# Parameter loads of the S5 and mixer parts behind later chunks' weights, the gate copy ahead of the rounding, tables and b blocks moved

## The chip, the cores and the metric

One core of a Trainium2 chip. A core has TensorE (PE, matrix products into PSUM), VectorE (DVE), ScalarE (ACT), GpSimd (POOL) and SyncE (SP), which here issues every DMA. Each engine runs its own list of instructions in order; they wait for each other by semaphores. The metric is the device time of one execution in microseconds (us), less is better.

## What is computed

A two-layer trunk over 256 positions of width 1024, in float32. Each layer has three sub-layers: a SwiGLU FFN, four token mixers side by side, and a second FFN:

```
mod = silu(c) @ ada_w[l] + ada_b[l]            # shift, scale, gate for each of 3 sub-layers
u = x*(1+scale0) + shift0;  x = LN(alpha*x + 0.5*gate0*(silu(u@w1)*(u@w3))@w2)
u = x*(1+scale1) + shift1;  x = LN(alpha*x + gate1*([A|B|C|D](u@w_in))@w_out)
u = x*(1+scale2) + shift2;  x = LN(alpha*x + 0.5*gate2*FFN(u))
```

Mixer D is an S5 state-space block. From its parameters (lam_re, lam_im, log_step, b_re, b_im, c_re, c_im) the kernel derives decays, tables of cosines and sines for 128 positions, and the matrices B and C. These depend on parameters alone, so they are worked out on DVE during the first FFN of the layer. Mixers A and B use sinks, w_uq and w_iq; mixer C uses the gate biases; D's output uses glu_w.

## The kernel before, in words

**The FFN.** Eleven chunks of 256 hidden columns (`CHUNKS`). Products are split: each float32 factor is a rounded part and a remainder, and PE does three products (high*high, high*low, low*high; lines 520 to 522 for the input weights, 545, 548, 549 for the output weights). For chunk c+1 the input weights come by DMA into a two-slot ring (`load_ffn_in`, 2 DMAs of 1 MB), ACT rounds them (`w_in_high`, L1610), DVE takes the remainder (`w_in_low`, L1013). The same goes for the output weights (`load_ffn_out`, `w_out_high` L1618, `w_out_low` L1018). The silu (ACT, L1603) and the product and split of h (DVE `ffn_tile`, L1002 to L1007) lie between PE's input and output matmuls. A chunk has two halves, ft = 0 and 1.

**adaLN blocks.** The modulation for later sub-layers is computed beside the FFN: in a chunk DVE multiplies a 2 MB block of `ada_w` by silu(c) in eight steps into `acc` (L935 or L938, and L941), and PE sums over partitions in the next chunk, before its output matmuls (L494 for columns, L503 for gates, which land in PSUM bank 7). ACT then copies a gate out (`copy_gate`, L1597). In layer 0 there is a block in each chunk 0 to 10 (the last in two halves, in chunk 10), in layer 1 in chunks 0 to 4 and 7 to 9.

**Orders around the change.** All orders are written out by hand.
- SP: weights of chunk 1, adaLN block, then 24 parameter DMAs on the semaphore `params_loaded` (L369 to L392), then `load_beside(0, ch)` for ch = 1 to 10: weights of chunk ch+1, each behind a wait for its ring slot, and the adaLN block of ch, behind a wait for DVE to have finished the block before. For ch = 9 in layer 0 SP also waits for the last table operation (`rot_step`), because half an adaLN block is loaded over the tables' scratch.
- PE: after chunk 1 it waits for the first gate and for all 24 parameter loads, and turns the rows of `prow` (L579). After chunk 10 it turns the b blocks (L586) and the c blocks (L593) and then the normalised x (L485).
- ACT in `ffn_chunk`: silu and input rounding of both halves, output rounding of the next chunk (behind a wait for PE's last matmul of this chunk), gate copy.
- DVE: behind each chunk's own work a piece of the S5 parameters: angles in 2, poles in 3, tables from 4 on (`TABLE_AT`; seven doubling steps of six operations), inverse in 4, gains in 5, `c_blocks` in 3 (layer 0) or 5 (layer 1), and `b_blocks` after the last h of chunk 10, in front of `deepnorm`. In layer 1 chunks 0 to 3 also carry the residual of the layer before (L1085, L1088).

## Time and profile before

| | us |
|---|---|
| median of 3 runs | 1149.54 (1148.61 to 1151.38) |
| profiled execution | 1149.38 |
| its span, first to last instruction | 1147.1 |
| PE busy | 1059.2 |
| DVE busy | 904.5 |
| ACT busy | 422.5 |

Times in the trace count from the first instruction of the span. A chunk of the first FFN takes PE close to 17.8 us. Layer 0's first FFN runs from about 38 to 250 us, layer 1's from about 601 to 797 us.

### The profile page before, as it was taken

How to read it: one execution, taken by the hardware profiler on the slowest of the kernel's cores; microseconds unless marked ns; L12 is line 12 of the kernel's file. 1: busy time of each engine (PE TensorE's matmuls, PEld its weight loads, DVE VectorE, ACT ScalarE, POOL GpSimd, SP SyncE). 2: the span in 40 equal slices, each digit the busy share in tenths (PEclk: the TensorE clock that was granted, in tenths of full speed). 3: DMA queues.
4: the chain of work that ended last, by engine and by line, in shares of the span. 5: the costliest groups of instructions: out<-in, count | busy, mean ns of one | idle time of the engine just before them, and what ended most of it. 6: DMA issues, size and time to landing. Idle time of an engine off the chain costs nothing.

```text
span 1147.1 us, 16956 instructions
## 1 busy us (share of the span) xinstructions
PE 1059.2 (92%) x6865; PEld 931.6 (81%) x6865; DVE 904.5 (79%) x1498; ACT 422.5 (37%) x566; POOL 38.9 (3%) x56
## 2 busy tenths in 40 slices
PE   1979999979999799999979999998899979999994
PEld 1869999967875599999969999997687549999994
DVE  6787999989975789878878898698697577755555
ACT  0435333311463333333333553332246243333330
POOL 1000000003000100000000000000300010000000
PEclk9999999988999899999989999999899989999997
DMA  9897989685251568888966886786134246654640
GB/s 367 266 313 259 330 277 307 225 219 187 80 199 57 183 236 313 290 274 308 330 231 186 300 282 217 255 316 153 73 128 165 92 157 210 220 180 155 217 147 37
DMA packets 184504, 250.82 MB, mean 219 GB/s; under 512 B 25372, under 2 KB 133216, under 8 KB 183404
## 3 DMA queue, kind: packets, MB, share of 16 engines
q1 hardware_dynamic: 184428, 249.76, 63.8%
q8 instruction: 54, 0.88, 0.3%
q14 instruction: 22, 0.18, 0.0%
HBM read 248.69 MB, written 1.05 MB: 218 GB/s over the span
## 4 chain that ended last, share of the span: by engine, by line
PE 82%; DVE 8%; SPq 5%; issue 2%; ACT 2%; DMA 1%; POOL 0%; POOLq 0%; DVEq 0%; ACTq 0%
PE PS L520 14%; PE PS L521 14%; PE PS L522 14%; PE PS L617 9%; PE PS L545 6%; PE PS L549 6%; PE PS L548 6%; PE PS L846 2%; PE PS L624 2%; PE PS L702 2%; SPq L323 2%; PE PS L494 1%; DVE stats L1062 1%; DVE xn L1057 1%; DVE xn L1050 1%
## 5 line engine op out<-in xcount | busy, mean ns | idle before, releaser
L520 PE MATMUL PS<-u_hi,w_in_hi 128*128 128x256 f32 x1408 | 400.3, 284 | 7.2 <-DVE u_lo L972 4.4
L522 PE MATMUL PS<-u_hi,w_in_lo 128*128 128x256 f32 x1408 | 400.5, 284 | 0.0
L521 PE MATMUL PS<-u_lo,w_in_hi 128*128 128x256 f32 x1408 | 400.0, 284 | 0.0
L520 PEld LDWEIGHTS PS<-u_hi,w_in_hi 128*128 128x128 f32 x1408 | 271.2, 193 | 10.1 <-issue 5.5
L521 PEld LDWEIGHTS PS<-u_lo,w_in_hi 128*128 128x128 f32 x1408 | 269.9, 192 | 1.6
L522 PEld LDWEIGHTS PS<-u_hi,w_in_lo 128*128 128x128 f32 x1408 | 269.5, 191 | 0.0
L1013 DVE TENSOR_TENSOR w_in_lo<-w_in_ring,w_in_hi 128x2048 fp32r<-128x2048 f32 x88 | 201.5, 2290 | 39.6 <-ACT w_in_hi L1610 39.5
L1610 ACT ACTIVATE w_in_hi<-w_in_ring 128x2048 fp32r<-128x2048 f32 x88 | 168.0, 1913 | 7.0 <-DMA w_in_ring<-in_ffn_w_dram 7.0
L941 DVE SCALAR_TENSOR_TENSOR acc<-arena,cs,acc 128x512 f32<-128x512 f32 x210 | 157.9, 752 | 7.5
L545 PE MATMUL PS<-w_out_hi,h_parts 128*128 128x512 f32 x352 | 146.6, 417 | 6.7 <-DVE h_parts L1007 6.6
L1618 ACT ACTIVATE w_out_hi<-w_out_ring 128x1024 fp32r<-128x1024 f32 x88 | 88.6, 1054 | 162.7 <-PE PS L549 162.7
L1603 ACT ACTIVATE arena<-PS 128x256 f32<-128x256 f32 x88 | 33.8, 384 | 300.3 <-PE PS L522 300.3
L549 PE MATMUL PS<-w_out_hi,h_parts 128*128 128x512 f32 x352 | 139.7, 397 | 0.0
L548 PE MATMUL PS<-w_out_lo,h_parts 128*128 128x512 f32 x352 | 139.5, 396 | 0.0
L1018 DVE TENSOR_TENSOR w_out_lo<-w_out_ring,w_out_hi 128x1024 fp32r<-128x1024 f32 x88 | 103.7, 1219 | 17.1 <-ACT w_out_hi L1618 16.9
L1002 DVE TENSOR_TENSOR arena<-arena,PS 128x256 f32<-128x256 f32 x88 | 36.8, 418 | 85.9 <-ACT arena L1603 85.8
L617 PE MATMUL PS<-uT,w_in_ring 128*128 128x256 f32 (+1 forms) x416 | 99.3, 397 | 3.6 <-ACT uT L1579 2.5
L617 PEld LDWEIGHTS PS<-uT,w_in_ring 128*128 128x128 f32 (+1 forms) x416 | 80.6, 197 | 20.0 <-issue 4.5
L545 PEld LDWEIGHTS PS<-w_out_hi,h_parts 128*128 128x128 f32 x352 | 66.8, 190 | 24.2 <-issue 10.7
L548 PEld LDWEIGHTS PS<-w_out_lo,h_parts 128*128 128x128 f32 x352 | 66.8, 190 | 16.6 <-issue 2.9
L549 PEld LDWEIGHTS PS<-w_out_hi,h_parts 128*128 128x128 f32 x352 | 66.9, 190 | 16.2
L1852 POOL TENSOR_TENSOR rstd<-var_eps,neg_half 128x1 f32<-128x1 f32 x12 | 10.5, 875 | 907.9 <-DVE var_eps L1067 907.9
(286 smaller groups left out, 988.1 us busy)
## 6 DMA issues: line engine op xcount, KB each, us to landing
w_in_ring<-in_ffn_w_dram SPq DMA_DIRECT2D x88, 1024.0 KB, 7.7
arena<-in_ada_w_dram SPq DMA_DIRECT2D x30, 2048.0 KB, 8.3
w_out_ring<-in_ffn_w_dram SPq DMA_DIRECT2D x44, 1024.0 KB, 6.5
w_in_ring<-in_w_in_dram SPq DMA_DIRECT2D x6, 1024.0 KB, 6.6
w_in_ring<-in_w_in_dram SPq DMA_DIRECT2D x10, 512.0 KB, 5.1
w_out_ring<-in_w_out_dram SPq DMA_DIRECT2D x4, 1024.0 KB, 10.6
w_in_ring<-in_w_in_dram SPq DMA_DIRECT2D x2, 2048.0 KB, 8.7
w_in_ring<-in_w_out_dram SPq DMA_DIRECT2D x4, 1024.0 KB, 5.9
```

The source lines that it names most:

```text
L520: pe.matmul(y, hi, u_hi[:, kt, :], start=(i == 0), stop=False)
L521: pe.matmul(y, hi, u_lo[:, kt, :], start=False, stop=False)
L522: mm = pe.matmul(y, lo[:, kt, half, :], u_hi[:, kt, :], start=False, stop=(i == KT - 1))
L545: mm = pe.matmul(y, h_hi, w_out_hi[ft][:, cols], start=(first and ft == 0), stop=False)
L548: pe.matmul(y, h_hi, w_out_lo[slot][:, ft, cols], start=False, stop=False)
L549: mm = pe.matmul(y, h_lo, w_out_hi[ft][:, cols], start=False, stop=(last and ft == 1))
L617: mm = pe.matmul(o[0:w, :], w_in_ring[(G_MIX + m) % 2][:, kt, c0:c0 + w], uT[:, kt, :], start=(kt == 0), stop=(kt == KT - 1))
L941: v.scalar_tensor_tensor(acc[:, :], part(buf, t), cs[:, t:t + 1], acc[:, :], ALU.mult, ALU.add).then_inc(sem("acc_step"), 1)
L1013: v.tensor_tensor(w_in_tile(w_in_lo, slot, ft), w_in_tile(w_in_ring, slot, ft), w_in_hi[ft][:, :, :, :].bitcast(F32), ALU.subtract).then_i ...
L1018: v.tensor_tensor(w_out_lo[slot][:, ft, :], w_out_ring[slot][:, ft, :], w_out_hi[ft][:, :].bitcast(F32), ALU.subtract).then_inc(sem("w_out ...
L1610: a.activation(w_in_hi[ft][:, :, :, :], w_in_tile(w_in_ring, slot, ft), ACT.Copy).then_inc(sem("w_in_high"), 1)
L1618: a.activation(w_out_hi[ft][:, :], w_out_ring[slot][:, ft, :], ACT.Copy).then_inc(sem("w_out_high"), 1)
```

## The change

The 24 parameter loads are split. Eleven (the rows of `prow` and `log_dt`) stay where they were. The four c loads go behind chunk loads 3 and 4 (two each), the two b loads behind 5 and 6, and the seven others (glu, uq, iq, sinks twice, two gate biases) behind 7. PE's transpose after chunk 1 waits for eleven loads only. Waits for all 24 are added in front of the mixer on PE, in `b_blocks`, `c_blocks`, in front of the sink logits on DVE and in front of the gate biases on ACT. ACT copies a gate before the output rounding and not after it. Each table step is done one chunk earlier, behind the poles in chunk 3; `c_blocks` and `b_blocks` are both done in chunk 9.

```diff
--- before.py
+++ after.py
@@ -73,7 +73,7 @@
 
 
 R_LNG, R_LNB, R_CW, R_CB, R_MHG, R_DS, R_GB, R_LR, R_LI, ROWS = 0, 24, 48, 64, 68, 70, 72, 74, 82, 90
-PARAM_DMAS = 24
+FIRST_PARAM_DMAS, PARAM_DMAS = 11, 24
 
 AW = 512
 BLOCKS = 9 * D // AW
@@ -377,22 +377,32 @@
                     sp.dma_start(log_dt[64 * half:64 * half + 64, :],
                                  log_step[L].rearrange("o (i two) -> two (o i)", two=2)[half:half + 1].to_broadcast([64, 8]),
                                  allow_slow_non_contiguous=True).then_inc(pl, 16)
-                for k, src in enumerate((b_re, b_im)):
-                    sp.dma_start(b_raw[:, k, :, :], src[L].rearrange("o (i two) p c -> (two p) (o i) c", two=2)).then_inc(pl, 16)
-                for k, src in enumerate((c_re, c_im)):
-                    for rep in range(2):
-                        sp.dma_start(c_blk[:, k, :, rep * 64:(rep + 1) * 64],
-                                     src[L].rearrange("o (t g) c p -> (g c) (o t) p", t=2)).then_inc(pl, 16)
-                sp.dma_start(glu_sb[:, :, :], glu_w[L].rearrange("o (t p) n -> p (o t) n", p=P)).then_inc(pl, 16)
-                sp.dma_start(uq_sb[:, :], w_uq[L].rearrange("o p n -> p (o n)")).then_inc(pl, 16)
-                sp.dma_start(iq_sb[:, :], w_iq[L].rearrange("o p n -> p (o n)")).then_inc(pl, 16)
-                for k in range(2):
-                    sp.dma_start(sinks_sb[:, k, :], sinks[L].to_broadcast([P, H])).then_inc(pl, 16)
-                for k, src in enumerate((ig_b, fg_b)):
-                    sp.dma_start(gate_bias[:, k:k + 1], src[L].rearrange("o h -> h o")).then_inc(pl, 16)
+                def load_blocks(k):
+
+                    if k < 2:
+                        for rep in range(2):
+                            sp.dma_start(c_blk[:, k, :, rep * 64:(rep + 1) * 64],
+                                         (c_re, c_im)[k][L].rearrange("o (t g) c p -> (g c) (o t) p", t=2)).then_inc(pl, 16)
+                    else:
+                        sp.dma_start(b_raw[:, k - 2, :, :], (b_re, b_im)[k - 2][L].rearrange("o (i two) p c -> (two p) (o i) c", two=2)
+                                     ).then_inc(pl, 16)
+
+                def load_mixer_params():
+
+                    sp.dma_start(glu_sb[:, :, :], glu_w[L].rearrange("o (t p) n -> p (o t) n", p=P)).then_inc(pl, 16)
+                    sp.dma_start(uq_sb[:, :], w_uq[L].rearrange("o p n -> p (o n)")).then_inc(pl, 16)
+                    sp.dma_start(iq_sb[:, :], w_iq[L].rearrange("o p n -> p (o n)")).then_inc(pl, 16)
+                    for k in range(2):
+                        sp.dma_start(sinks_sb[:, k, :], sinks[L].to_broadcast([P, H])).then_inc(pl, 16)
+                    for k, src in enumerate((ig_b, fg_b)):
+                        sp.dma_start(gate_bias[:, k:k + 1], src[L].rearrange("o h -> h o")).then_inc(pl, 16)
 
                 for ch in range(1, CHUNKS):
                     load_beside(0, ch)
+                    if 3 <= ch < 7:
+                        load_blocks(ch - 3)
+                    if ch == 7:
+                        load_mixer_params()
                 sp.wait_ge(sem("x_ready"), l * 6 + 2)
                 waited(sp)
                 load_ln(l, 0)
@@ -575,7 +585,7 @@
                     ffn_chunk(l, 0, c)
                     if c == 1:
                         pe.wait_ge(sem("gate_ready"), (1, 8)[l])
-                        pe.wait_ge(sem("params_loaded"), (l + 1) * (16 * PARAM_DMAS))
+                        pe.wait_ge(sem("params_loaded"), 16 * (l * PARAM_DMAS + FIRST_PARAM_DMAS))
                         pe.transpose(PS[:, 7, 0:ROWS], prow[:, :], ident[0:ROWS, 0:ROWS]).then_inc(sem("prm_turned"), 1)
                 release_out(0)
 
@@ -704,6 +714,7 @@
                     if k == 1:
                         pe.drain().then_inc(sem(f"w_out_used{g % 2}"), 1)
 
+                pe.wait_ge(sem("params_loaded"), (l + 1) * 16 * PARAM_DMAS)
                 chunk_in(0)
                 z_feature("ud0", 0, 0)
                 z_feature("cq", 0, 256)
@@ -1164,6 +1175,7 @@
 
                 def b_blocks():
 
+                    v.wait_ge(sem("params_loaded"), (l + 1) * 16 * PARAM_DMAS)
                     kre = S5["k_re"].unsqueeze(2).to_broadcast([P, 8, 16])
                     kim = S5["k_im"].unsqueeze(2).to_broadcast([P, 8, 16])
                     bt = [qk_tanh[:, k * P:(k + 1) * P].rearrange("p (i c) -> p i c", c=16) for k in range(4)]
@@ -1180,6 +1192,7 @@
 
                 def c_blocks():
 
+                    v.wait_ge(sem("params_loaded"), (l + 1) * 16 * PARAM_DMAS)
                     for k, sign in ((0, 1.0), (1, -1.0)):
                         v.scalar_tensor_tensor(c_blk[:, k, :, :], c_blk[:, k, :, :], sign,
                                                block_mask[:, :].unsqueeze(1).to_broadcast([P, 2, P]), ALU.mult, ALU.mult
@@ -1207,21 +1220,24 @@
                             v.wait_ge(sem("rot_step"), at + 4)
                             v.tensor_tensor(sin_t[:, :, hi], t4[2], t4[3], ALU.add).then_inc(sem("rot_step"), 1)
 
-                TABLE_AT = {4: ((0, range(6)), (1, range(6))), 5: ((2, range(6)), (3, range(6))), 6: ((4, range(6)),),
-                            7: ((5, range(6)),), 8: ((6, range(0, 3)),), 9: ((6, range(3, 6)),)}
+                TABLE_AT = {3: ((0, range(6)), (1, range(6))), 4: ((2, range(6)), (3, range(6))), 5: ((4, range(6)),),
+                            6: ((5, range(6)),), 7: ((6, range(0, 3)),), 8: ((6, range(3, 6)),)}
 
                 for c in range(CHUNKS - 1):
                     ffn_chunk(l, 0, c)
                     if l and c < 4:
                         residual(l - 1, 2, c)
+                    if c == 3:
+                        s5_poles()
                     for k, ops in TABLE_AT.get(c, ()):
                         table_ops(k, ops)
                     if c == 4:
                         s5_inverse()
                     if c == 5:
                         s5_gains()
-                    if c == (3, 5)[l]:
+                    if c == 9:
                         c_blocks()
+                        b_blocks()
                     if c == 0 and l == 0:
                         bias_constants()
                     if c == 1:
@@ -1229,8 +1245,6 @@
                         v.tensor_copy(prm[:, :], PS[:, 7, 0:ROWS]).then_inc(sem("prm_ready"), 1)
                     if c == 2:
                         s5_angles()
-                    if c == 3:
-                        s5_poles()
 
                 tile = ff_tile(l, 0, CHUNKS - 1)
                 for ft in range(2):
@@ -1239,7 +1253,6 @@
                     if l == 0:
                         ada_block(10, None, "ada_halves_loaded", ft + 1, acc_2, ts=range(4 * ft, 4 * ft + 4))
                     ffn_tile(ft, tile)
-                b_blocks()
                 assert step[0] == STEPS
                 if l == 0:
                     mod_cols(2, 4, 6, 8, 10)
@@ -1432,6 +1445,7 @@
                                                ALU.mult, ALU.add).then_inc(sem("conv_step"), 1)
 
                 s5_rotate_out(1)
+                v.wait_ge(sem("params_loaded"), (l + 1) * 16 * PARAM_DMAS)
                 sk = sinks_sb[:, :, :].rearrange("p t h -> p (t h)")
                 v.wait_ge(sem("consts_ready"), 8)
                 logits(bias_a, work[2], "sa_ready", "sa_read", mx_a, nmx_a, "a", sk)
@@ -1629,8 +1643,10 @@
                             a.wait_ge(sem(f"w_in_loaded{1 - slot}"), in_loads(l, ff_group(f, c + 1)))
                         w_in_high(1 - slot, ft, tile + (2 + ft))
                 if not last:
+                    if c - 1 in ADA[l, f] and gate_of(ADA[l, f][c - 1]) is not None:
+                        copy_gate(ADA[l, f][c - 1])
                     w_out_high(l, f, c + 1)
-                if c - 1 in ADA[l, f] and gate_of(ADA[l, f][c - 1]) is not None:
+                elif c - 1 in ADA[l, f] and gate_of(ADA[l, f][c - 1]) is not None:
                     copy_gate(ADA[l, f][c - 1])
 
             evac_uT(0, 0, 1, 0, lambda: w_in_high(0, 0, 0))
@@ -1717,6 +1733,7 @@
                 z_copies("ka", [(kaT[64 * k:64 * k + 64, t, :], 64 * t, 64 * t + 64) for t in range(2) for k in range(2)])
                 a.wait_ge(sem("x_ready"), l * 6 + 4)
                 a.wait_ge(sem("gates_turned"), l + 1)
+                a.wait_ge(sem("params_loaded"), (l + 1) * 16 * PARAM_DMAS)
                 for k in range(2):
                     a.activation(rows[:, k, :], PS[0:H, 6, k * T:(k + 1) * T], ACT.Identity, bias=gate_bias[:, k:k + 1]
                                  ).then_inc(sem("gates_read"), 1)
```

## Rows read from the trace of the kernel before

**Rows 1.** The page: busy time, share of the span and instructions of each engine.
```profile
PE 1059.2 (92%) x6865; PEld 931.6 (81%) x6865; DVE 904.5 (79%) x1498; ACT 422.5 (37%) x566; POOL 38.9 (3%) x56
```

**Rows 2.** Chain of waits: start us, us, what; layer 0's first sub-layer.
```profile
61.79 8.77 DMA w_in_ring<-in_ffn_w_dram
...
185.59 0.86 PE PS L503 x2
203.34 0.86 PE PS L503 x2
```

**Rows 3.** Order of SP: start us, us spent issuing, line, what; [idle, releaser] in all orders.
```profile
44.47 2.42 SPq L381 DMA_DIRECT2D b_raw<-in_b_re_dram  x1
...
61.35 1.02 SPq L323 DMA_DIRECT2D w_in_ring<-in_ffn_w_dram  x2
...
64.75 0.76 SPq L293 DMA_DIRECT2D arena<-in_ada_w_dram  x1
...
168.97 1.00 SPq L323 DMA_DIRECT2D w_in_ring<-in_ffn_w_dram  x2
```

**Rows 4.** Order of ACT in layer 0: start us, us, line, operation.
```profile
70.58 1.92 ACT L1610 ACTIVATE w_in_hi<-w_in_ring 128x2048 fp32r<-128x2048 f32 x1 [7.05 <-DMA w_in_ring<-in_ffn_w_dram]
...
82.67 0.57 ACT L1597 ACTIVATE gate_bc<-PS 128x512 f32<-128x512 f32 x1
...
180.24 1.91 ACT L1610 ACTIVATE w_in_hi<-w_in_ring 128x2048 fp32r<-128x2048 f32 x1
```

**Rows 5.** Order of PE in chunks 0 to 2 of layer 0.
```profile
51.72 0.39 PE L545 MATMUL PS<-w_out_hi,h_parts 128*128 128x512 f32 x1
...
68.62 1.02 PE L503 MATMUL PS<-acc,ones 128*128 128x512 f32 x2
...
76.09 0.47 PE L545 MATMUL PS<-w_out_hi,h_parts 128*128 128x512 f32 x1 [3.67 <-DVE h_parts L1007]
...
83.30 0.30 PE L579 MATMUL PS<-ident,prow 90*128 90x90 f32 x1 [2.64 <-ACT gate_bc L1597]
...
96.35 1.02 PE L503 MATMUL PS<-acc,ones 128*128 128x512 f32 x2
```

**Rows 6.** Windows: stretch, length, busy us of each engine, PEclk, DMA share, GB/s.
```profile
76.00:84.00 8.00, 5.28 (x18) 3.88 (x19) 7.36 (x8) 3.22 (x4) 0.00 (x0) 0.78 1.09 360
```

**Rows 7.** Order of DVE at the adaLN block of chunk 1, layer 0.
```profile
78.57 0.75 DVE L935 SCALAR_TENSOR_TENSOR acc<-arena,cs,gate_bias_row 128x512 f32<-128x512 f32 x1 [0.43 <-DMA arena<-in_ada_w_dram]
```

**Rows 8.** Windows, same columns, while layer 1's parameters are loaded.
```profile
604.00:608.00 4.00, 4.00 (x28) 4.00 (x27) 4.00 (x4) 0.04 (x1) 0.00 (x0) 0.73 0.13 9
```

**Rows 9.** Order of DVE in chunks 4 and 5 of layer 1.
```profile
684.39 0.43 DVE L1007 TENSOR_TENSOR h_parts<-arena,h_parts 128x256 fp32r<-128x256 f32 x1
...
696.17 0.17 DVE L1202 TENSOR_TENSOR rot_flat<-cos_t 128x8 f32<-128x8 f32 x1
...
697.62 0.16 DVE L1149 TENSOR_TENSOR s5p<-prm 128x8 f32<-128x8 f32 x1
...
707.77 0.19 DVE L1202 TENSOR_TENSOR rot_flat<-cos_t 128x32 f32<-128x32 f32 x1
...
711.10 0.76 DVE L1184 SCALAR_TENSOR_TENSOR c_blk<-c_blk,block_mask 128x256 f32<-128x256 f32 x2
```

**Rows 10.** Order of PE: first output matmul of chunk 4, layer 1.
```profile
685.84 0.80 PE L545 MATMUL PS<-w_out_hi,h_parts 128*128 128x512 f32 x1
```

**Rows 11.** Order of DVE at the first deepnorm of either layer.
```profile
243.69 0.28 DVE L1170 TENSOR_TENSOR qk_tanh<-b_raw,s5p 128x128 f32<-128x128 f32 x1
...
246.33 1.29 DVE L1050 TENSOR_TENSOR xn<-PS,gate_bc 128x512 f32<-128x512 f32 x2
...
795.21 1.29 DVE L1050 TENSOR_TENSOR xn<-PS,gate_bc 128x512 f32<-128x512 f32 x2
```

**Rows 12.** Order of PE: the matmul that finishes the second bank, either layer.
```profile
245.84 0.63 PE L549 MATMUL PS<-w_out_hi,h_parts 128*128 128x512 f32 x1
...
793.89 0.39 PE L549 MATMUL PS<-w_out_hi,h_parts 128*128 128x512 f32 x1
```

## The prediction, made before the changed kernel was run

> **What bounds the kernel now.** I read the page first, then the chain of waits, then the orders of SP, PE, ACT and DVE around each place that the diff touches. TensorE is busy for 1059.2 of 1147.1 us [rows 1]. In the first sub-layer (the FFN's eleven chunks) the chain is PE's own work, one chunk every 203.34 - 185.59 = 17.75 us [rows 2]. So the change can pay only where PE waits, and cost only where it makes PE wait. PE's waits near the touched code are three: chunk 1 of layer 0, and the turn from the FFN to the mixer in each layer, where the chain runs over DVE.
>
> The wait in chunk 1 starts at SP. SP begins the thirteen loads that move at 44.47 us and issues chunk 2's first weights behind them, at 61.35 [rows 3]. These land as 61.79 + 8.77 = 70.56 [rows 2]. ACT rounds them in program order between the two silus of chunk 1: it was free 7.05 us before, at 63.53 [rows 4]. DVE stands behind ACT, the second half of h comes late, and PE waits 3.67 us at 76.09. When PE has finished, it waits once more, 2.64 us to 83.30, for the gate copy [rows 5], which ACT runs at 82.67, after the output weights' rounding, and that itself waits for PE's last matmul of the chunk [rows 4]. The granted clock is 1.0 before, and 0.78 on average from 76 to 84 us, after the 3.67 us wait [rows 6]: part of that stretch ran at 1.2 GHz.
>
> **The start of layer 0 (gain).** Without the thirteen loads SP comes to chunk 2's weights at 44.47 and waits for their ring slot, which PE gives back with its first output matmul of chunk 0, at 51.72 [rows 5]. With the slow landing of before (70.58 - 61.35 = 9.2 us [rows 3, 4]) they are there at 61.2, 2.3 us ahead of ACT's 63.53. Before, h's second half was there 76.09 - 70.58 = 5.5 us after ACT began; 5.5 after 63.53 is 69.0, but its silu waits for PE's last input matmul (68.6) and some 2.5 us of silu, weight difference and products follow: 71.2. PE wants it at 76.09 - 3.67 = 72.4: no wait. The gate sum is done by PE at the start of chunk 1's output, so ACT copies the gate at about 71.5 instead of 82.67, and the transpose at 83.30 follows PE's last matmul directly. What is late next? The adaLN block of chunk 1 is issued when DVE has finished block 0, at 62.5; with its old landing time (it was waited for until 78.57 after an issue at 64.75, 13.8 us [rows 3, 7]) it is there at 76.4, DVE finishes its eight steps (6.2) at 82.6 and, with the parameter copy (0.2), the output weights' differences (2.3) and the products (1.1), chunk 2's first h at 86.2. PE wants that half a us after its sum at 86.5 (68.62 + 17.85, below), at 86.9. That is the thinnest cover here, 0.7 us, with the old landing time as the bad end; it lands amid less traffic now, so I take no wait.
> The sum: PE's gate or column sum opens each chunk's output part at 68.62 in chunk 1 and 96.35 in chunk 2 [rows 5], 27.73 us apart. Undisturbed it is 17.75 plus 0.10 for the transpose: 17.85. Gain 9.88 us: 6.31 of waits and 3.57 of slow clock. Bounds: 6.3 if the clock falls all the same, and 9.9, since nothing more is lost there.
>
> **The moved loads where they now stand.** Four c loads behind chunks 3 and 4, b_re and b_im one each behind 5 and 6, seven small ones behind 7. Each follows its chunk's adaLN block, some 8 us ahead of the next weights. They are not free: from 604 to 608 us, when nothing but the b loads of layer 1 was left to move, the 16 DMA engines were busy for 0.13 at 9 GB/s [rows 8], and that state held for some 8.5 us, so 4.3 us of queue for each b load. Weights issued behind one would land up to 4.3 us later. Chunk 8's weights are issued at 168.97 and ACT wants them at 180.24 [rows 3, 4]: 11.3 us, and with an ordinary 7 us to land 4.3 us are left, just the size of the hold; ACT's result is wanted by DVE only 1 us after that. In layer 1 chunks 5 and 6 have no adaLN load. I take 0; the other end is one stall like that of chunk 1.
> The Trainium skill, page "DMA: Bandwidth & Descriptors", section "Why a DMA increments its semaphore by 16 and not by 1", says that one DMA is spread over the largest number of engines up to 16 that divides the slowest dimension of both sides; for b that dimension is 2 in the source, so two engines of 16, 0.125, and the trace's 0.13 agrees. By that rule the weights' sixteen-engine DMAs are held on two engines for the whole of a b load and the rest can't help, which makes the sum the other end above; if b were spread like the weights the hold would be far below 4.3 us.
>
> **Tables one chunk back (DVE).** A pair of table steps costs 697.62 - 696.17 = 1.45 us; the second pair takes 12 instructions of about 0.19, some 2.1 us [rows 9]. Layer 0: chunk 3 gains 1.45 and loses the c masks (0.76 with its end, 0.68 until the next operation starts [rows 9]), chunk 4 gains 0.7, and h has some 2 us of cover there: nothing. Layer 1 has no cover: DVE runs the residual as well. Chunk 3 gets +1.45. Chunk 4's first h was ready at 684.39 + 0.43 = 684.82 and PE used it at 685.84 [rows 9, 10]; now 686.27, a wait of 0.4. DVE runs without a pause there, so its second h comes 3.3 us after the first, and PE's matmuls on the first take 3.2: another 0.1. In chunk 5 DVE is later by 2.1 in all (the next pair goes in where the first one was), h's second half comes 0.4 after the moved PE. Together +1.0 us (bounds 0 and 2.1, all that DVE is late). Chunk 5 has no adaLN block in layer 1 and DVE recovers.
>
> **b blocks and c masks in chunk 9.** The b blocks (8 instructions, about 1.97 us, from 243.69) stood between the last h and deepnorm [rows 11]. Chunk 9 loses the last three table operations (1.93) and gets c masks and b blocks (0.68 + 1.97): +0.72 in both layers.
> Layer 0: DVE is the bound in chunk 10, because two halves of an adaLN block stand in it. So the last h and PE's last output matmuls come 0.72 later. Deepnorm began at 246.33, after the b blocks. Now DVE is free at 245.1, but its second multiply needs the bank that PE finished at 245.84 + 0.63 = 246.47 [rows 11, 12], now 247.2, where DVE had started it at 246.93. Net +0.3 (bounds -1.25, all that DVE is free earlier, and +0.72).
> Layer 1: no adaLN block in chunk 10; DVE waited for PE in front of the last h, which hides the +0.72. DVE is free 1.97 earlier, 793.2 instead of 795.21 [rows 11]. PE's second bank is done at 793.89 + 0.39 = 794.28 [rows 12], the second multiply stood at 795.81: -1.4. What is late next is ACT, whose copies of the turned blocks follow PE and not DVE: they may push the first normalisation, but the chain ends with the second, 3.8 us later, which has room.
> The half block that waited for the last table is issued 17 us earlier, and with it the mixer's first weights; PE did not wait for either, so 0. The new waits for all 24 loads stand 15 us or more behind the last load: 0.
>
> Sum: -9.88 + 1.0 + 0.3 - 1.4 = -9.98, near 10 us. The profiled execution took 1149.38 (span 1147.1 and 2.3 around it); that is 1139.4. The median of the runs is 1149.54, 0.16 above it: I say 1139.5.
>
> **Rivals.**
> 1. The start pays only in part: weights or the adaLN block land later than I let them. For: 0.7 us of cover. Against: SP issues less. About 2 us of wait return: 1141.5. Chance 0.08.
> 2. A b load holds weights once in layer 0. A whole stall like chunk 1's is 3.67 plus up to 3.57 of slow clock, 7.2 us; a partial one 2. 1141.5 to 1146.7. Chance 0.12.
> 3. The gate wait does not go (it was for the loads, not the copy). The copy ended at 83.25 and PE went on at 83.30, which speaks against it. 2.64 and a part of the slow clock, 4.2: 1143.7. Chance 0.05.
> 4. Slower: the b loads hold weights in both layers, at chunks 7 and 8, four places of 7.2 us. It decides from the second whole stall on: 14.4 - 10 = +4.4, 1154. For: each hold is as long as the room. Against: it needs the long landing as well, and the chunks of layer 1 have no adaLN traffic ahead. Chance 0.05.
> 5. It doesn't do what it says: chunk 2's weights can't come earlier since their slot is not free. SP would wait at 52, so this needs a slot given back 9 us later than PE's order has it. 1149. Chance 0.03.
> The forecast has 0.67, with 1137.5 to 1142 for itself. The range 1136.8 to 1145 takes in rivals 1 and 3 and most of 2. A change of 0.3%, 3.4 us, is what a measurement can tell from none: faster 0.92, same 0.03, slower 0.05.
>
> **What would show it.** After: chunk 2's weights issued at about 52 and no wait of ACT for them; no 3.67 and 2.64 us waits of PE; the sums of chunks 1 and 2 17.85 us apart at clock 1.0; PE's chunk 4 of layer 1 waiting about 0.5 us for h; the first multiply of deepnorm after PE's bank and not after b blocks. Wrong: ACT waiting for weights of chunks 7 or 8, or the sums still more than 20 us apart.

## The result and the profile after

The changed kernel takes 1138.45 us (median of 4 runs, 1137.98 to 1139.63) against 1149.07 us for the kernel before, run beside it (4 runs, 1146.81 to 1151.38): a ratio of 0.991, 95% interval 0.9893 to 0.9927. A second set of runs of the same kernel gave 1137.91 (4 runs) against 1148.3, ratio 0.9904 (0.9888 to 0.9921). The forecast was 1139.5. The profiled execution took 1138.35 us, its span 1136.1.

The page after, busy time of each engine. PE's work is the same count of matmuls and 5.8 us shorter than in [rows 1], which fits less of it running at the lower clock; the span is 11.0 us shorter:

```profile
PE 1053.4 (93%) x6865; PEld 926.9 (82%) x6865; DVE 904.4 (80%) x1498; ACT 422.4 (37%) x566; POOL 38.9 (3%) x56
```

Order of SP after (start us, us spent issuing, line, what), for [rows 3]. Chunk 2's weights are issued at 51.70 instead of 61.35; the first moved load stands behind chunk 3's adaLN block:

```profile
42.99 1.31 SPq L377 DMA_DIRECT2D log_dt<-in_log_step_dram  x2
51.70 1.02 SPq L323 DMA_DIRECT2D w_in_ring<-in_ffn_w_dram  x2
...
62.13 0.58 SPq L293 DMA_DIRECT2D arena<-in_ada_w_dram  x1
...
97.28 1.68 SPq L384 DMA_DIRECT2D c_blk<-in_c_re_dram  x1
```

Order of ACT after, for [rows 4]. The 7.05 us wait is now 1.45, and the gate is copied at 70.45 instead of 82.67:

```profile
64.51 1.93 ACT L1624 ACTIVATE w_in_hi<-w_in_ring 128x2048 fp32r<-128x2048 f32 x1 [1.45 <-DMA w_in_ring<-in_ffn_w_dram]
...
70.45 0.58 ACT L1611 ACTIVATE gate_bc<-PS 128x512 f32<-128x512 f32 x1
```

Order of PE after, for [rows 5]: the gate sums of chunks 1 and 2 and the transpose between them. Neither wait is there, and the sums stand 17.88 us apart instead of 27.73:

```profile
68.16 1.02 PE L513 MATMUL PS<-acc,ones 128*128 128x512 f32 x2
...
74.56 0.24 PE L589 MATMUL PS<-ident,prow 90*128 90x90 f32 x1
...
86.04 1.02 PE L513 MATMUL PS<-acc,ones 128*128 128x512 f32 x2
```

Windows after (stretch, length, busy us of PE, PEld, DVE, ACT, POOL, granted clock, DMA share, GB/s), for [rows 6]: the granted clock that was 0.78 is 1.00.

```profile
76.00:84.00 8.00, 8.00 (x70) 8.00 (x69) 7.43 (x11) 5.80 (x6) 0.00 (x0) 1.00 0.95 328
```

The two turns to the mixer, order of DVE after, for [rows 11]. In both layers the first multiply now waits for PE's bank instead of standing behind the b blocks:

```profile
235.39 1.29 DVE L1061 TENSOR_TENSOR xn<-PS,gate_bc 128x512 f32<-128x512 f32 x2 [0.58 <-PE PS L559]
...
784.22 1.29 DVE L1061 TENSOR_TENSOR xn<-PS,gate_bc 128x512 f32<-128x512 f32 x2 [0.77 <-PE PS L559]
```

Where the 11.03 us of span went, by PE's own landmarks (distance between the same two matmuls, after minus before): up to chunk 1's sum -0.46; chunk 1 to chunk 2, -9.85; the end of layer 0's first part and the turn to the mixer, -0.69; the start of layer 1, +0.21; its chunks 4 and 5, +0.93; its turn to the mixer, -1.17. Chunk 1's sum stands anywhere between 66.9 and 69.0 us over all the kernels below, so the first term is start-up spread. A "sum" here is PE's sum of an adaLN block, which opens a chunk's output part; "layer 0's stretch" below is the distance from chunk 10's sum to the first sum of the mixer.

### The profile page after: what moved, and what is told of

It is laid out like the page before. It is cut to its first block, busy times and chain, and to the rows that moved or that the text cites. A ratio compares the mean times of both kernels' runs of the same rounds, so it can differ in the third digit from the quotient of the medians.

```text
span 1136.1 us, 16957 instructions
## 1 busy us (share of the span) xinstructions
PE 1053.4 (93%) x6865; PEld 926.9 (82%) x6865; DVE 904.4 (80%) x1498; ACT 422.4 (37%) x566; POOL 38.9 (3%) x56
## 4 chain that ended last, share of the span: by engine, by line
PE 83%; DVE 10%; issue 2%; ACT 2%; DMA 2%; SPq 0%; POOL 0%; POOLq 0%; DVEq 0%; ACTq 0%
PE PS L530 14%; PE PS L531 14%; PE PS L532 14%; PE PS L627 9%; PE PS L555 6%; PE PS L559 6%; PE PS L558 6%; PE PS L857 2%; PE PS L634 2%; PE PS L712 2%; DVE acc L952 2%; DMA xn<-in_ada_w_dram 2%; PE PS L504 1%; DVE stats L1073 1%; DVE xn L1068 1%
```

## Experiments

Twelve runs were made, in four groups (eleven other kernels, and the changed one again), each group beside the kernel before on one chip (that was 1149.02, 1149.77, 1148.3 and 1148.56 us). "Distance" is always from chunk 1's to chunk 2's sum in layer 0: 27.73 before, 17.88 after, 17.75 for an undisturbed chunk.

**1. The loads alone.** The changed kernel with the gate copy where it was:

```
-                    if c - 1 in ADA[l, f] and gate_of(ADA[l, f][c - 1]) is not None:
-                        copy_gate(ADA[l, f][c - 1])
                     w_out_high(l, f, c + 1)
-                elif c - 1 in ADA[l, f] and ...:
+                if c - 1 in ADA[l, f] and ...:
                     copy_gate(ADA[l, f][c - 1])
```

> The changed kernel with one part undone: ACT copies the gate after the output weights' rounding again. Theory (the wait at PE's transpose is for the copy, and the copy is late since the rounding waits for PE): PE waits 2.6 us before the transpose after chunk 1 of layer 0, and the gate sums of chunks 1 and 2 are 20.5 us apart if the clock stays at 1.0, up to 22 if it falls after the wait (17.88 in the changed kernel); nothing else moves: 1141.0 to 1142.5 us. Rival (the wait was for the parameter loads): no wait, 17.9 us apart, 1138.5 us.

**2. The gate copy alone**: the kernel before with only that edit the other way round.

> The kernel before with the gate copy alone moved ahead of the rounding. Theory: the 2.64 us wait before the transpose goes, the 3.67 us wait for h in chunk 1 stays, and since the clock still falls after it the sums are 23.5 to 25.1 us apart instead of 27.7: 1145.0 to 1146.5 us. Rival (both waits are one and the same lateness of the weights, so that the gain comes only with the loads): the sums stay above 27 us apart, 1149 us.

Measured: the loads alone 1142.63 us (4 runs), ratio 0.9946 (0.9928 to 0.9964); the copy alone 1144.69 (10 runs), ratio 0.9964 (0.9952 to 0.9976). Order of PE, the loads alone:

```profile
66.89 1.02 PE L513 MATMUL PS<-acc,ones 128*128 128x512 f32 x2
...
72.10 0.47 PE L555 MATMUL PS<-w_out_hi,h_parts 128*128 128x512 f32 x1 [1.42 <-DVE h_parts L1018]
...
77.75 0.30 PE L589 MATMUL PS<-ident,prow 90*128 90x90 f32 x1 [2.64 <-ACT gate_bc L1611]
...
90.81 1.02 PE L513 MATMUL PS<-acc,ones 128*128 128x512 f32 x2
```

Order of PE, the copy alone:

```profile
67.64 1.02 PE L503 MATMUL PS<-acc,ones 128*128 128x512 f32 x2
...
76.25 0.72 PE L545 MATMUL PS<-w_out_hi,h_parts 128*128 128x512 f32 x1 [4.82 <-DVE h_parts L1007]
...
92.13 1.02 PE L503 MATMUL PS<-acc,ones 128*128 128x512 f32 x2
```

Each leaves the other's wait: the 2.64 us behind the output matmuls go with the copy and stay with the loads alone, so rival 3 is dead. The distances are 23.92 and 24.49, that is 3.81 and 3.24 gained, while together they gain 9.85. For the first I had expected 20.5 to 22 us and 1142.5 at most, without its 1.42 us wait; the second's distance is inside its 23.5 to 25.1, and its time just under the 1145.0 expected. What each distance has over 17.75, in us: PE's two waits, and the rest, which is the slow clock and some 0.1 of transpose.

| | waits | rest |
|---|---|---|
| before | 6.31 | 3.67 |
| loads alone | 4.06 | 2.11 |
| copy alone | 4.82 | 1.92 |
| both | 0 | 0.13 |

So of the 2.8 us that neither gets alone, 2.6 are waits: 1.42 us for h that the first has and the profiled changed kernel has not, and 1.15 us by which the second's wait is longer than the 3.67 of before. The slow clock goes in two nearly equal parts, with the first wait and with the last.

The 1.42 us come from ACT. Its order in the first of the two:

```profile
66.60 1.92 ACT L1624 ACTIVATE w_in_hi<-w_in_ring 128x2048 fp32r<-128x2048 f32 x1 [4.80 <-DMA w_in_ring<-in_ffn_w_dram]
```

Its weights were issued at 50.48 and came 16.1 us later. In the changed kernel it is 12.8 (51.70 to 64.51), in its second profile 14.9 (50.80 to 65.74), there with a PE wait of 0.25. Over the seven profiles with log_dt in this place they were issued between 50.48 and 52.59 and taken between 64.34 and 66.60: 11.8 to 16.1 us, by and large the longer the earlier they were issued. I had taken 9.2. What holds them?

**3. b loads alone deferred** (the kernel before with b_re and b_im behind chunks 5 and 6, PE's transpose waiting for the other 22), and **4. both b loads behind chunk 5** in the changed kernel:

```
                 for ch in range(1, CHUNKS):
                     load_beside(0, ch)
+                    if ch in (5, 6):                      # 3: in the kernel before
+                        sp.dma_start(b_raw[:, ch - 5, :, :], ...).then_inc(pl, 16)
...
+                    if ch == 5:                           # 4: in the changed kernel
+                        load_blocks(2)
+                        load_blocks(3)
```

> The kernel before with only the two b loads taken from SP's list and put behind chunks 5 and 6; c and mixer loads, gate copy, tables and b blocks as before. Theory of the prediction (the b loads hold the queue, 4.3 us each): the c loads are issued without delay, SP comes to chunk 2's weights near 52, the 3.67 us wait goes, the gate wait stays: sums 20.5 to 22 us apart, 1142 to 1143.5 us. Rival (the two log_dt loads hold one DMA engine for about 8 us, as the share of 0.05 from 590 to 598 us in the changed kernel suggests, and SP is blocked on that engine's ring): the first c load still blocks for some us and the weights are issued at 54 to 58; little of the 3.67 us wait may be left all the same.

> The changed kernel with both b loads behind chunk 5 (c loads behind 3 and 4, the seven others behind 7, as changed). Theory of the prediction (4.3 us of queue for each b load): 8.6 us of hold ahead of chunk 7's weights, which are issued 8 us later; they land about 7 us late, ACT waits for them some 3 us in chunk 6 of layer 0 and PE up to 3 us: 1138.5 to 1143. Rival (a b load costs the queue 2 us or less, and what held it was log_dt): no wait of ACT for weights there, 1138.5 us, no difference from the changed kernel.

Measured: 1143.94 us (6 runs), ratio 0.996 (0.9945 to 0.9975), and 1139.89 (4 runs), ratio 0.9918 (0.9899 to 0.9937). Order of SP in the first, where no b load stands in front of the weights:

```profile
42.92 1.31 SPq L377 DMA_DIRECT2D log_dt<-in_log_step_dram  x2
44.27 3.44 SPq L382 DMA_DIRECT2D c_blk<-in_c_re_dram  x2
47.75 2.38 SPq L382 DMA_DIRECT2D c_blk<-in_c_im_dram  x2
...
50.69 2.95 SPq L385 DMA_DIRECT2D uq_sb<-in_w_uq_dram  x1
...
57.05 1.02 SPq L323 DMA_DIRECT2D w_in_ring<-in_ffn_w_dram  x2
```

The weights go out 4.3 us earlier than the 61.35 of before, for both b loads and not for each; the other 5.35 us to the changed kernel's 51.70 are the c and the seven small loads. SP is still held behind log_dt: issuing uq takes it 2.95 us here and 0.61 in the changed kernel at 170.12, c_im 2.38 against 1.14. ACT waits 3.02 us for the weights (to 66.69) and PE no longer for h: the 3.67 us are gone with the b loads alone, the gate's 2.64 stay, and the distance is 22.19, a little over the 20.5 to 22 expected, with 1.80 of slow clock.

In the other kernel the two b loads went out at 132.10 and 132.79 (the second kept SP for 3.72 us), chunk 7's weights at 140.08, and ACT took those at 151.32 without a wait, against the 3 us of the theory. So b loads do occupy the queue for a few us, but not up to the next weights. Two lines of windows of the changed kernel show one by itself: b_re went out at 682.49 in layer 1, beside megabytes of weights, and by 688 nothing was left to move:

```profile
686.00:688.00 2.00, 2.00 (x20) 2.00 (x19) 1.82 (x10) 0.30 (x2) 0.00 (x0) 1.00 0.57 120
688.00:690.00 2.00, 2.00 (x20) 2.00 (x19) 1.76 (x12) 1.89 (x2) 0.00 (x0) 1.00 0.01 1
```

Windows of the changed kernel at the parameter loads of layer 1, where log_dt went out at 583.59 and no b load is near (same columns as above):

```profile
592.00:594.00 2.00, 2.00 (x11) 2.00 (x11) 2.00 (x4) 1.04 (x2) 0.00 (x0) 0.50 0.05 0
594.00:596.00 2.00, 2.00 (x15) 2.00 (x14) 2.00 (x2) 0.00 (x0) 0.00 (x0) 0.73 0.05 0
596.00:598.00 2.00, 2.00 (x19) 2.00 (x18) 2.00 (x2) 0.00 (x0) 0.00 (x0) 1.00 0.03 0
```

A near-empty state like that of [rows 8], which I put down to the b loads, is here without them, from 590 until 598, 14 us after log_dt's issue. And the 0.13 of [rows 8] is a mean of unlike parts. The same stretch in the kernel before, by 2 us:

```profile
604.00:606.00 2.00, 2.00 (x12) 2.00 (x11) 2.00 (x2) 0.04 (x1) 0.00 (x0) 0.50 0.07 3
606.00:608.00 2.00, 2.00 (x18) 2.00 (x18) 2.00 (x3) 0.00 (x0) 0.00 (x0) 0.97 0.20 14
```

Log_dt is two loads of 512 separate 4-byte numbers each.

**5. log_dt behind chunk 2's weights**, in the changed kernel, counted apart from the other parameters, with ACT's exponential waiting for them:

```
                 for ch in range(1, CHUNKS):
                     load_beside(0, ch)
+                    if ch == 1:
+                        for half in range(2):
+                            sp.dma_start(log_dt[64 * half:64 * half + 64, :], ...)
```

> The changed kernel with log_dt's two small loads issued behind chunk 2's weights, on a semaphore of their own. Theory (the two loads of 4-byte elements hold one of the 16 engines for some 8 us, and the weights behind them wait for that one): chunk 2's weights land about 7 us after their issue instead of 12.8, ScalarE's wait of 1.45 us for them goes, the stretch at 5 to 15% DMA share moves from 50 to 56 us to behind chunk 2's weights, and chunk 3's weights, issued 15 us later, land as before. The time stays 1138.5 within 0.4 us, since TensorE did not wait for these weights. Rival (the weights are slow by themselves, being many small rows at a busy time): they land 12.8 us after their issue again.

Measured: 1145.65 us (7 runs), ratio 0.9967 (0.9956 to 0.9978). Order of SP:

```profile
63.85 1.41 SPq L400 DMA_DIRECT2D log_dt<-in_log_step_dram  x2
70.02 6.07 SPq L323 DMA_DIRECT2D w_in_ring<-in_ffn_w_dram  x2
76.20 5.22 SPq L331 DMA_DIRECT2D w_out_ring<-in_ffn_w_dram  x1
```

Windows, order of ACT and order of PE there:

```profile
70.00:76.00 6.00, 6.00 (x31) 5.00 (x30) 5.83 (x9) 2.21 (x3) 0.00 (x0) 1.00 0.10 18
```

```profile
88.23 1.92 ACT L1625 ACTIVATE w_in_hi<-w_in_ring 128x2048 fp32r<-128x2048 f32 x1 [3.71 <-DMA w_in_ring<-in_ffn_w_dram]
```

```profile
86.55 1.02 PE L514 MATMUL PS<-acc,ones 128*128 128x512 f32 x2
...
93.75 0.47 PE L556 MATMUL PS<-w_out_hi,h_parts 128*128 128x512 f32 x1 [3.39 <-DVE h_parts L1019]
```

The place of the hold moved with log_dt, as said: chunk 2's weights are no longer waited for, and chunk 3's are, which ACT takes 18.2 us after issue. ACT also waits 3.98 us, until 81.33, for log_dt itself, and in layer 1 until 637.48 after an issue at 620.55: 17.5 and 16.9 us from issue to landing, the only direct measures of it. That the time would stay was wrong: log_dt was put six us ahead of weights that were needed, where it had stood nine us ahead of them. PE lost 5.2 us between the sums of chunks 2 and 3 of layer 0 and 4.2 at the same place of layer 1.

**6. log_dt in one piece**: 16 adjacent numbers for each partition, 128 pieces of 64 bytes, and two half-height exponentials that pick the even and the odd ones:

```
-        log_dt = sb("log_dt", [P, 8])
+        log_dt = sb("log_dt", [P, 16])
...
-                                 log_step[L].rearrange("o (i two) -> two (o i)", two=2)[half:half + 1].to_broadcast([64, 8]),
-                                 allow_slow_non_contiguous=True).then_inc(pl, 16)
+                                 log_step[L].to_broadcast([64, 16])).then_inc(pl, 16)
```

> The changed kernel with log_dt loaded as 16 adjacent numbers per partition (128 pieces of 64 bytes instead of 1024 of 4 bytes) and the even and odd ones picked by two half-height exponentials instead of one. Theory (the count of small pieces is what holds an engine and the queue): the stretch at a DMA share of 5 to 15% from 50 to 56 us goes, chunk 2's weights land some 7 to 10 us after their issue instead of 12.8, ScalarE does not wait for them, and the same in layer 1. One more ScalarE instruction of 0.2 us. The time stays at 1138.5 within 0.5 us, since TensorE did not wait there. Rival (the broadcast over the partitions is slow, whatever the pieces): share and landing stay.

Measured: 1143.58 us (6 runs), ratio 0.9955 (0.9939 to 0.9971), beside the second set of the changed kernel at 1137.91. The two kernels in the window where that load was in flight, first this one, then the changed kernel:

```profile
52.00:54.00 2.00, 2.00 (x11) 1.60 (x10) 1.37 (x3) 1.10 (x1) 0.00 (x0) 1.00 0.70 212
54.00:56.00 2.00, 2.00 (x10) 1.64 (x9) 2.00 (x2) 0.00 (x0) 0.00 (x0) 1.00 1.08 374
```

```profile
52.00:54.00 2.00, 2.00 (x10) 1.60 (x9) 1.33 (x4) 1.60 (x1) 0.00 (x0) 1.00 0.27 19
54.00:56.00 2.00, 2.00 (x10) 1.63 (x9) 2.00 (x2) 0.00 (x0) 0.00 (x0) 1.00 0.31 48
```

The hold is gone: the queue runs at full rate 3 us after the weights' issue (51.21), and ACT takes them at 62.52 with no wait. So log_dt's 4-byte pieces are the cause of this hold, and the broadcast, which is still there, is not; whether it is their number, their size or the gaps between them in memory, this run does not tell apart. Yet the time rose by 5.7 us, and not there: an undisturbed feed-forward chunk takes 17.88 to 17.94 us, in every part of the program, instead of 17.74 to 17.84. The last experiment below is about that.

**7. The tables back, 8. the b blocks back, 9. the blocks apart.** The changed kernel with layer 1's tables one chunk later; with b_blocks after the last h; and the first of these with layer 0's c and b blocks in chunks 7 and 8:

```
+                if l:                                              # 7 and 9
+                    TABLE_AT = {c + 1: k for c, k in TABLE_AT.items()}
...
-                        b_blocks()                                 # 8: in chunk 9
...
+                b_blocks()                                         # 8: after the last h
...
-                    if c == 9:                                     # 9
+                    if c == (7, 9)[l]:
                         c_blocks()
+                    if c == (8, 9)[l]:
                         b_blocks()
```

> The changed kernel with layer 1's rotation tables one chunk later, where they stood before (4 to 9 instead of 3 to 8). Theory: of the 0.93 us that layer 1's chunks 4 and 5 lost, all is the tables ahead of chunk 3's and 4's last h tiles, so the distance from chunk 2's sum to chunk 5's sum in layer 1 goes from 54.11 back to some 53.3 us, and the time from 1138.45 to about 1137.5 us. The price: VectorE gets 1.93 us more in chunk 9, so that its h tile for chunk 10 comes at 781.3 us of the changed kernel's clock instead of 779.4, just when TensorE wants it (781.4): a wait of 0 to 0.3 us. Rival (the 0.93 us is start-up spread or b_im's load in chunk 6): the distance stays 54.1 us and the time 1138.5.

> The changed kernel with the b blocks again after the last h tile, the c blocks staying in chunk 9. Theory: layer 1's end gives its 1.17 us back (the first multiply behind the last matmul starts 1.97 us later), so this kernel is about 1.2 us slower there; in layer 0 the last h tile comes 1.97 us earlier, TensorE's wait of 2.51 us before it shrinks to about 0.6 us, and VectorE then does the b blocks before the first multiply, which comes out within 0.5 us of where it is: about 1139.6 us in all. Rival (the 1.17 us come from elsewhere in the end of the layer): the stretch from chunk 10's sum to the transposes behind it in layer 1 stays at 49.5 us and the time at 1138.5.

> The previous kernel but one (tables of layer 1 as before the change) and, in layer 0 alone, the c blocks in chunk 7 and the b blocks in chunk 8; layer 1 keeps both in chunk 9. Theory: in layer 0 VectorE's last h tiles are late by the blocks that stand in chunk 9, 2.69 us; with them out of chunks 9 and 10 TensorE's wait of 2.51 us before the last output tile goes, if chunks 7 and 8 have room for 0.72 and 1.97 us. Layer 0's end gets 1.6 to 2.5 us shorter, and with layer 1's 0.9 us the time is about 1136. Rival (chunks 7 and 8 of layer 0 are as tight as chunk 9, for VectorE works without a gap through them): the lateness is carried along, the wait stays 2.5 us, and the time is 1137.5 as with the tables alone.

Measured: 1138.79 us (4 runs), ratio 0.9901 (0.9885 to 0.9917); 1135.16 (5 runs, 1134.41 to 1139.79), ratio 0.9887 (0.9869 to 0.9905); 1134.35 (4 runs, 1131.73 to 1136.59), ratio 0.9868 (0.985 to 0.9887).

With the tables back, layer 1's stretch from chunk 2's to chunk 5's sum is 53.32 us instead of 54.11, and 53.28 before: 0.79 of the 0.93 us is theirs, the theory's way. The price was as forecast too: from chunk 10's sum of layer 1 to the transposes behind the mixer's start it is 49.80 us, against 49.49 and 49.30 in the two profiles of the changed kernel. The whole time can't show what is left, 0.5 us being under a third of the interval's half width. The profiled execution was even 1.5 us longer, and 1.0 of that is in layer 0's stretch, where this kernel is the changed one to the letter. Order of PE at the last h there, and windows behind it; first with the tables back, then the changed kernel:

```profile
235.23 0.76 PE L555 MATMUL PS<-w_out_hi,h_parts 128*128 128x512 f32 x1 [2.52 <-DVE h_parts L1018]
```

```profile
235.00:237.00 2.00, 1.77 (x4) 1.49 (x5) 0.67 (x7) 0.00 (x0) 0.00 (x0) 0.50 0.99 123
```

```profile
234.33 0.47 PE L555 MATMUL PS<-w_out_hi,h_parts 128*128 128x512 f32 x1 [2.51 <-DVE h_parts L1018]
```

```profile
234.00:236.00 2.00, 1.67 (x7) 1.42 (x8) 1.35 (x7) 0.00 (x0) 0.00 (x0) 1.00 1.06 142
```

The same code, the same wait to a hundredth, and once the granted clock is 0.50 (1.2 GHz) and once 1.00 (2.4 GHz). From chunk 10's sum to the mixer's first sum of this layer that makes 45.73 us in the one and 44.72 in the other; from chunk 10's sum to PE's transpose of the b blocks alone, 11.95 and 10.53.

With the b blocks back, the same stretch of layer 1 (sum to transposes) is 50.38 us against 49.49 in the changed kernel and 49.30 in its second profile: +0.9 to 1.1 where I expected 1.17. In layer 0 PE's wait for the last h is 1.47 instead of 0.79 + 2.51, and the stretch 44.53 against 44.72. These two stretches thus say about 0.7 us slower; but its whole span is 1135.8, as in the changed kernel's two profiles (1136.1 and 1135.5), and its median of 1135.16 is far under the 1139.6 expected, on 5 runs that spread over 5.4 us. The interval just holds the changed kernel's second ratio, 0.9904, and not its first, 0.991. For the whole time this one is inconclusive, and that the b blocks' new place is worth something in the whole is not shown.

With the blocks apart, layer 0's stretch is 42.55 us, 2.17 under the changed kernel, inside the 1.6 to 2.5 forecast: chunks 7 and 8 had the room, PE's waits of 0.79 and 2.51 shrink to one of 1.77 (I had written that it goes), and the clock stays at 1.00. Layer 1 keeps the 0.8 of the tables and pays 0.3 at its end.

**10. The changed kernel again, 11. blocks apart with log_dt in one piece, 12. the same with addresses kept.** The last differs from the one before it in two lines:

```
-        log_dt = sb("log_dt", [P, 16])
+        log_dt_unused = sb("log_dt_unused", [P, 8])
...
         small = sb("small", [P, 32, 8])
+        log_dt = sb("log_dt", [P, 16])
```

> The changed kernel once more, beside the next two on one chip, for the blocks apart and for the short loads of log_dt to be compared with it. It should come out at 1138.5 within 1 us. Where its profile shows the wait of 2.51 us for the last h tile of layer 0's first feed-forward part, the clock behind it is either 1.00 or 0.5 to 0.6; the stretch from chunk 10's sum to the turn of the b blocks is 10.5 us in the first case and 11.4 to 12.0 in the second, as in the runs so far.

> The kernel with layer 1's tables as before, layer 0's c and b blocks in chunks 7 and 8, and log_dt loaded in one piece. Theory: the blocks apart are worth 2.2 us in layer 0 and 0.8 in layer 1 over the changed kernel, less 0.3 at layer 1's end, and the short loads nothing: 1135.5 to 1136 us, or 2.6 us under the changed kernel run beside it. Rival (the runs of the blocks apart were low by chance): less than 1 us under it.

> The previous kernel (blocks apart, log_dt in one piece) with its 16-wide buffer placed behind all others in SBUF and the old 8-wide one left where it was, unused, so that every other buffer has the address that it has in the kernel before the change. Theory (the chunks of 17.90 to 17.93 us instead of 17.75 to 17.84, in every feed-forward part, come from the 32 bytes by which the wider buffer shifted the operands behind it): the chunks go back to 17.75 and 17.84, TensorE's matmuls on u_lo from 285 to 283 ns, and the time from 1139.9 to about 1135.5 us. Rival (the added ScalarE instruction or another change of the program does it): chunks of 17.9 and 1140 us again.

Measured: the changed kernel 1137.91 us, with the clock behind the 2.51 us wait at 1.00 and 10.54 us from chunk 10's sum to the transpose of the b blocks, the first of the two cases; blocks apart with the wider buffer 1139.86 (6 runs), ratio 0.9923 (0.9909 to 0.9937); with the addresses kept 1135.22 (5 runs, 1131.43 to 1136.39), ratio 0.9873 (0.9856 to 0.9891). Groups of PE's instructions (busy us, mean ns), the matmuls on u_lo, first with the addresses shifted, then kept:

```profile
L530 PE MATMUL PS<-u_lo,w_in_hi 128*128 128x256 f32 x1408 | 401.5, 285 | 0.0
```

```profile
L531 PE MATMUL PS<-u_lo,w_in_hi 128*128 128x256 f32 x1408 | 398.4, 283 | 0.0
```

The program is the same and only addresses differ: chunks go back from 17.93 to 17.83 us and the time by 4.6 us (4.2 in the profiled spans, about 4 of them the 44 chunks' tenth each). The two ran on different chips, but the changed kernel on the first one's chip had the short chunks too. All three groups of input products are slower, also the ones that read neither u_lo nor anything else that moved (u_hi with w_in_lo, 286 against 283 ns); with matmuls that overlap, these means don't single out an operand. By the order of the buffers only u_lo, w_in_hi and w_out_hi among the feed-forward's operands lie behind log_dt and moved. The theory of the 32 bytes holds, the run before, 1139.86 where 1135.5 to 1136 was expected, is explained by it, and the blocks apart are worth what was forecast: this kernel and the ninth, at ratios 0.9873 and 0.9868, are the fastest of the study, about 0.3% under the changed kernel's 0.9904 and 0.991. Between these two, log_dt's form makes no difference that the runs can tell.

## Why the prediction was right

- **The start of layer 0, -9.88 forecast, -9.85 measured.** Both waits and the slow clock went (6.31 and 3.54 of 6.31 and 3.57), and the two waits were shown apart in the first three experiments. The time came out right because this term is nearly all of the sum.
- **Within that step the landing time was wrong.** I took 9.2 us from the kernel before and concluded 2.3 us of cover for ACT. It is 11.8 to 16.1, and ACT waited 0.39 to 4.8 us, 1.45 in the profiled run. That PE did not wait there was room behind ACT that I had not counted on, and in part luck: 0.25 us of it reached PE in the second profile, and 1.42 in the first experiment, where PE had started earliest. The landing of before was short because SP had been held at the loads behind log_dt until 61.35, by when log_dt's 13 to 17.5 us were over. The adaLN block, which I had called the thinnest cover, was not waited for in the profiled run and for 0.45 us by DVE in the second profile, which did not reach PE.
- **"4.3 us of queue for each b load" was wrong in its cause.** Most of [rows 8] is log_dt's hold: a share of 0.07 until 606, much as the 0.05 without any b load. It was issued 9 us ahead of that stretch (594.67 in the kernel before) and takes 13 to 17.5 us wherever it stands: from 42.99 to about 56 and from 583.59 to about 598 in the changed kernel, from 63.85 to 81.33 in the fifth experiment. The b loads cost SP 4.3 us for the two. My conclusion for the b loads, 0, held; had log_dt been among the moved loads, the fifth experiment shows the cost that I had bounded as a stall like chunk 1's: 5.2 us in layer 0 and 4.2 in layer 1. The Trainium skill, page "DMA: Bandwidth & Descriptors", section "Why a DMA increments its semaphore by 16 and not by 1", on which I had leaned for b, would put log_dt, as I read its patterns, on sixteen engines, for the slowest dimension is 64 on both sides. For b I read that rule on a doubtful dimension: in the source the step of `two` is 64 times that of `p`, so that both can be carried as one dimension of 128, and the agreement of 0.125 with 0.13 was chance, since 0.13 is the mean of 0.07 and 0.20. The trace shows shares of 0.05 to 0.07 for many us, as of one engine of sixteen, or of sixteen that mostly wait; which of the two, no run here tells. What decides is that the pieces are small (sixth experiment), which that rule leaves out.
- **Tables, +1.0 forecast, +0.93 measured**, of which 0.79 went when they went back.
- **End of layer 0, +0.3 forecast, -0.69 measured.** The wait for the last h is 2.51 us both before and after, and the lateness that I priced at 0.72 shows as a new wait of 0.79 for the h before it, which none of the three profiles with the old order has. What I had not in the sum is that the clock behind that wait falls in some executions and not in others. Compared at equal clock the step was right: with a fallen clock the stretch is 45.41, 45.41 and 45.08 us in the three kernels with the old order, and 45.61 and 45.73 with the new one, +0.4; without a fall it is 44.32 to 44.72 with the new order (four profiles). The part from chunk 10's sum to the transpose of the b blocks, which holds the wait and the clock behind it, is 11.27 to 11.39 us with the old order and fallen clock, 11.84 to 12.10 with the new order and fallen clock, and 10.46 to 10.54 without a fall, so the fall costs about 1.4 us there. The fifth experiment belongs to the fallen ones (12.10); its whole stretch is short, 44.30, for another reason: behind the transpose of the b blocks it has 32.20 us where the changed kernel has 34.19 and 33.99, and its clock falls later at the transposes of x. All three profiles with the old order show the fall, and three of seven with the new order and the wait of 2.51 us; whether that is chance or the order's doing stays open.
- **End of layer 1, -1.4 forecast, -1.17 measured**; its size is confirmed by taking it back (0.9 to 1.1).

Over the profiled pair the span is 11.0 us shorter, 1.0 more than forecast: 0.99 at layer 0's end, where the clock did not fall, and 0.25 of spread at the starts of the two layers, less 0.23 that layer 1's end gave short.

## What to carry to other kernels

Find what holds a queue by what was issued last before it went quiet, not by what is largest: here 4 KB in four-byte pieces took 13 to 17.5 us, where a load of 1 MB takes 7.7, and it costs what stands close behind it. Look at a share by short windows before putting it down to one load. A wait on TensorE cost more than its length here: with one or both left of the two that followed one another, 1.8 to 3.7 us of slow clock came on top. And compare stretches between fixed instructions, at equal granted clock, before believing a difference of one or two us in a whole time.

## What the runs showed of the hardware that was not expected

- Two loads of 512 four-byte numbers each hold the issuing queue for 13 to 17.5 us: the weights behind them are there 11.8 to 18.2 us after issue instead of at most 11.3 (51.21 to 62.52, log_dt in one piece), and the issue of a later DMA blocks SP for up to 6.07 us. As 128 pieces of 64 bytes the same numbers cost nothing that shows: the DMA share is 0.00 from 50 to 52 us where it is 0.05 with the small pieces.
- After the same wait of 2.51 us on the same code TensorE's granted clock fell to 0.50 in three profiles and stayed at 1.00 in four, for 1.0 us of layer 0's stretch between the two shown and 1.4 us of its first part. Such places may make a good part of the spread of 2 to 5 us between runs of one kernel; that was not counted out.
- A shift of 32 bytes in the SBUF addresses of some operands (u_lo, w_in_hi and w_out_hi among them) made TensorE's input products slower (283 to 285 or 286 ns), each chunk longer by 0.1 us, and the program by 4.6 us. Which buffer it is was not tried.
